# Rows of three feed-forward chunks and four attention pairs are moved as words into tiles of the rounded type before TensorE transposes them

## The reference, cut to what matters

```python
def swiglu(h, w1, w3, w2):                       # three times in all; hidden width 2816
    return (jax.nn.silu(h @ w1) * (h @ w3)) @ w2

def stick_breaking_attention(q, k, v):           # 16 heads of 64, blocks of 128 queries
    ...
        z = jnp.einsum('bthd,bshd->bhts', qb, k).astype(jnp.float32) * (HEAD_DIM ** -0.5)
        brk = jnp.where(strict, jax.nn.softplus(z), 0.0)
        ...
        log_a = jax.nn.log_sigmoid(z) - remain
        a = jnp.where(strict, jnp.exp(log_a), 0.0).astype(v.dtype)
        o = jnp.einsum('bhts,bshd->bthd', a, v)
```

## Time and profile before

| what | value |
|---|---|
| median of three runs | 950.38 us |
| profiled execution | 951.45 us |
| its span | 949.6 us |
| PE busy | 941.2 us, 99% of the span |
| DVE busy | 793.8 us, 84% |
| ACT busy | 578.3 us, 61% |
| granted TensorE clock | 1.00 |

### The profile page before, as it was taken

How to read it: one execution, slowest core, us unless ns; L and a number is a source line. 1 busy time by engine, 2 the same in 40 slices (tenths; PEclk the granted TensorE clock), 3 DMA queues, 4 the chain that set the end, 5 groups by cost and what they waited for, 6 DMA issues and landing times.

```text
span 949.6 us, 12028 instructions
## 1 busy us (share of the span) xinstructions
PE 941.2 (99%) x4705; PEld 785.0 (83%) x4705; DVE 793.8 (84%) x836; ACT 578.3 (61%) x609; POOL 86.9 (9%) x94
## 2 busy tenths in 40 slices
PE   7999999999999999999999999999999999999998
PEld 7877888888889888888888888888888888888887
DVE  4888999989856877999989888965885779999996
ACT  6666676665654655676666666565744456665672
POOL 3611101101010000101101023001010001101010
PEclk9999999999999999999999999999999999999999
DMA  8746888785457437879786367457255485987751
GB/s 297 269 134 202 253 295 236 190 298 134 145 125 249 153 114 220 244 249 259 202 278 164 114 155 251 171 181 218 94 199 196 165 273 141 318 236 208 255 133 44
DMA packets 125993, 191.32 MB, mean 201 GB/s; under 512 B 7353, under 2 KB 87617, under 8 KB 125937
## 3 DMA queue, kind: packets, MB, share of 16 engines
q1 hardware_dynamic: 110992, 172.59, 54.7%
q0 software_dynamic: 14640, 17.77, 10.6%
q10 hardware_dynamic: 304, 0.20, 0.1%
HBM read 189.49 MB, written 1.05 MB: 201 GB/s over the span
## 4 chain that ended last, share of the span: by engine, by line
PE 98%; ACT 1%; DMA 0%; DVE 0%; issue 0%; DVEq 0%
PE psum L2153 27%; PE psum L2154 26%; PE psum L2158 26%; PE psum L2297 4%; PE psum L2146 2%; PE psum L2148 2%; PE psum L2147 2%; PE psum L2671 1%; PE psum L2682 1%; PE psum L2672 1%; PE psum L2705 1%; PE psum L2731 1%; ACT arena L944 1%; PE psum L2334 0%; DMA cst<-consts 0%; PE psum L2314 0%
## 5 line engine op out<-in xcount | busy, mean ns | idle before, releaser
L1416 DVE TENSOR_TENSOR low<-raw,high 128x2048 fp32r<-128x2048 f32 (+1 forms) x109 | 245.4, 2253 | 60.2 <-ACT high L874 60.2
L874 ACT ACTIVATE high<-raw 128x2048 fp32r<-128x2048 f32 (+1 forms) x112 | 211.6, 1890 | 90.5 <-PE psum L2158 68.0
L2153 PE MATMUL psum<-high,xh 128*128 128x512 f32 x596 | 237.0, 398 | 0.0
L2154 PE MATMUL psum<-high,xl 128*128 128x512 f32 x596 | 232.6, 390 | 0.0
L879 ACT ACTIVATE high<-arena 128x2048 fp32r<-128x2048 f32 x88 | 168.7, 1917 | 75.9 <-PE psum L2158 72.2
L1422 DVE TENSOR_TENSOR low<-arena,high 128x2048 fp32r<-128x2048 f32 x88 | 200.7, 2286 | 11.1 <-ACT high L879 11.0
L2158 PE MATMUL psum<-low,xh 128*128 128x512 f32 x596 | 155.4, 390 | 0.0
L2153 PEld LDWEIGHTS psum<-high,xh 128*128 128x128 f32 x596 | 112.0, 188 | 23.3 <-issue 0.7
L2158 PEld LDWEIGHTS psum<-low,xh 128*128 128x128 f32 x596 | 111.6, 188 | 23.7 <-issue 0.3
L2154 PEld LDWEIGHTS psum<-high,xl 128*128 128x128 f32 x596 | 112.0, 188 | 22.1
L2153 PE MATMUL psum<-high,mh 128*128 128x512 f32 x256 | 102.1, 399 | 0.0
(11 more groups left out here) (241 smaller groups left out, 1185.6 us busy)
## 6 DMA issues: line engine op xcount, KB each, us to landing
raw<-in_ffn_w SPq DMA_DIRECT2D x68, 512.0 KB, 6.3
arena<-in_ffn_w SPq DMA_DIRECT2D x64, 512.0 KB, 7.0
raw<-in_w_in SPq DMA_DIRECT2D x50, 512.0 KB, 4.7
raw<-in_od_w_qkv SPq DMA_DIRECT2D x24, 512.0 KB, 5.0
raw<-in_w_ffn_down SPq DMA_DIRECT2D x22, 512.0 KB, 5.7
arena<-in_ffn_w POOLq DMA_DIRECT2D x16, 512.0 KB, 7.6
arena<-in_w_ffn_gate SPq DMA_DIRECT2D x16, 512.0 KB, 6.7
arena<-in_w_ffn_up SPq DMA_DIRECT2D x16, 512.0 KB, 8.2
```

The source lines that it names most:

```text
L874: nc.scalar.activation(high[:, n % RING, 0:cols], raw[:, r, 0:cols], ACT.Copy).then_inc(high_ready, 1)
L1416: nc.vector.tensor_tensor(low[:, n % RING, 0:cols], raw[:, RING_AT[n] % RING, 0:cols], high[:, n % RING, 0:cols].bitcast(F32), ALU.subtrac ...
L2153: nc.tensor.matmul(out, sh, wh, start=start, stop=False, skip_group_check=True)
L2154: nc.tensor.matmul(out, sl, wh, start=False, stop=False, skip_group_check=True)
```

## The change

Three feed-forward chunks (1, 6, 7, in each of the three feed-forwards) and four of the eight pairs of the stick-breaking attention (0, 1, 2, 6) are no longer transposed as fp32. SP copies their rows bit for bit into a tile of type fp32r (`words`, and `a_words`, which lies in the feed-forward's `gh`, idle at that time), and PE transposes that tile against `identr`, an fp32r copy of the identity that ACT makes once, ahead of the first feed-forward. The transposes themselves stay 128x128, four or six in a group.

Some of them stand elsewhere now. `hiddenT(1)` goes from in front of product 5 to behind product 2 of the first pair, `hiddenT(7)` from in front of product 5 to behind product 6 of the last, and `stick_aT` of pairs 0, 1, 2 and 6 goes from the start of unit 7+p to unit 8 (start), 8, 9 and 13 (in the middle, behind eight products of the unit). DVE's product of the next pair waits for the copy of this one instead of its transposes. Apart from that, the three semaphores of the constants become one, and so do those of the identity and the first gain.

```diff
+        MOVED_CHUNKS = (1, 6, 7)
...
-        A_T_BEFORE = {7 + p: p for p in range(8)}
+        A_T_BEFORE = {8: 0, 10: 3, 11: 4, 12: 5, 14: 7}
+        A_T_MID = {8: 1, 9: 2, 13: 6}
+        MOVED = (0, 1, 2, 6)
...
+            def move_a(p):
+
+                sp.wait_ge(a_ready, p + 1)
+                if p != MOVED[0]:
+                    sp.wait_ge(aT_ready, MOVED[MOVED.index(p) - 1] + 1)
+                sp.dma_start(a_words.bitcast(F32), o_a).then_inc(a_moved, 16)
...
+                def move_hidden(c):
+
+                    if c in PLAIN:
+                        sp.wait_ge(hidden_ready, 2 * plain_seq(f, c) + 2)
+                    else:
+                        sp.wait_ge(pair_hidden, 4 * pair_seq(f, c) + 4)
+                    before = MOVED_CHUNKS.index(c)
+                    if before:
+                        sp.wait_ge(hiddenT_ready, down_seq(f, MOVED_CHUNKS[before - 1]) + 1)
...
+                    for t in range(NT):
+                        sp.dma_start(words[:, t, :].bitcast(F32), hidden_of(c)[t]).then_inc(hidden_moved, 16)
...
                 load_down(f, 1)
+                move_hidden(1)
...
                 load_x21(7)
+                move_hidden(6)
...
                 load_down(f, 10)
+                move_hidden(7)
...
                 if n == U_Q:
-                    load_consts("bands", "bands", bands_in)
+                    load_consts("bands", "bands", masks_in)
                 if n == U_Q + 1:
-                    load_consts("rope", "rope", rope_in)
+                    load_consts("rope", "rope", masks_in)
...
+                if n - U_QKV[0] - 11 in (0, 1, 2):
+                    move_a(n - U_QKV[0] - 11)
...
+            nc.scalar.activation(identr[:], ident, ACT.Copy).then_inc(identr_ready, 1)
             ffn(0)
...
             dve.wait_ge(idx_w_copied, 2)
-            dve.wait_ge(masks_in, 16)
+            dve.wait_ge(masks_in, 16 * 3)
...
+                if p - 1 in MOVED:
+                    dve.wait_ge(a_moved, 16 * MOVED.index(p - 1) + 16)
+                elif p:
                     dve.wait_ge(aT_ready, p)
...
+                    if c in MOVED_CHUNKS:
+                        pe.wait_ge(hidden_moved, chunks_moved(f, c))
+                        pe.wait_ge(identr_ready, 1)
+                        for k in range(2):
+                            for t in range(NT):
+                                j = NT * k + t
+                                ins = nc.tensor.transpose(bank(6, j * P, (j + 1) * P).bitcast(F32R), words[:, t, k * P:(k + 1) * P], identr[:])
...
                 def products_6_2_3(p):
...
                     product(p, 6, bank(7), sum_tile(2), True, False)
+                    if p == LAST_PAIR:
+                        hiddenT(7)
                     pe.wait_ge(s1_ready, pairs_done(f, p))
                     product(p, 2, bank(0), x_tile(0, 1), False, True)
+                    if p == FIRST_PAIR:
+                        hiddenT(1)
...
-                pe.wait_ge(a_ready, p + 1)
+                if p in MOVED:
+                    pe.wait_ge(a_moved, 16 * MOVED.index(p) + 16)
+                    pe.wait_ge(identr_ready, 1)
+                else:
+                    pe.wait_ge(a_ready, p + 1)
```

More of the change, by code:

```diff
@@ L255, in program @@
         cst = sb("cst", [P, DECAY_AT])
+        identr = sb("identr", [P, P], F32R)
+        words = sb("words", [P, NT, FC], F32R)
         selbias = sb("selbias", [P, TRI])
@@ L359, in program @@
         o_a = take(2 * TRI).rearrange("p (e n) -> p e n", e=2)
+        a_words = gh.rearrange("p a b n -> p (a b n)")[:, 0:2 * TRI].rearrange("p (e n) -> p e n", e=2)
         A_RING = 4
@@ L386, in program @@
         r_o = xn
-        ident_in, masks_in, bands_in, rope_in = sem("ident_in"), sem("masks_in"), sem("bands_in"), sem("rope_in")
+        ident_in, masks_in = sem("ident_in"), sem("masks_in")
         decay_in = sem("decay_in")
         x_in = [[sem(f"x_in{t}_{q}") for q in range(2)] for t in range(NT)]
-        first_gain_in, gains_in = sem("first_gain_in"), sem("gains_in")
+        gains_in = sem("gains_in")
         first_gain_T, first_gain_ready = sem("first_gain_T"), sem("first_gain_ready")
@@ L448, in program @@
         stored, last_read = sem("stored"), sem("last_read")
+        identr_ready, a_moved, hidden_moved = sem("identr_ready"), sem("a_moved"), sem("hidden_moved")
         def bank(b, c0=0, c1=512):
@@ L572, in hidden_of, with chunks_moved @@
             return (f_half, f_C21[:, 0:FC]) if c in PAIRS else (f_C12[:, 0:FC], f_C22[:, 0:FC])
+        MOVED_CHUNKS = (1, 6, 7)
+        def chunks_moved(f, c):
+            return 32 * (len(MOVED_CHUNKS) * f + MOVED_CHUNKS.index(c) + 1)
         def landed_count(n):
@@ L666, in load_x21 @@
                     up_quarter(f, X21, p, 1, x21_in)
+                def move_hidden(c):
[6 more added lines that the diff above has]
+                        sp.wait_ge(hiddenT_ready, down_seq(f, MOVED_CHUNKS[before - 1]) + 1)
+                    elif f:
+                        sp.wait_ge(hiddenT_ready, down_seq(f - 1, MOVED_CHUNKS[-1]) + 1)
+                    for t in range(NT):
+                        sp.dma_start(words[:, t, :].bitcast(F32), hidden_of(c)[t]).then_inc(hidden_moved, 16)
                 load_up(f, 0, 0)
+                if f == 1:
+                    move_a(6)
                 load_up(f, 0, 1)
@@ L1143, in _ @@
             act.dma_start(ident, consts[:, 0:P]).then_inc(ident_in, 16)
[L1144 removed]
+            act.dma_start(gains[0:KD, 0:P], NORM_G[0].rearrange("(k p) -> k p", k=KD)).then_inc(ident_in, 16)
             def first_x_high(kk):
@@ L1277, in _ @@
                     stick_sigmoids(WEIGHTS_AT[u])
+                if u in A_T_MID:
+                    stick_aT(A_T_MID[u])
                 if u:
@@ L2047, in _ @@
                     s = chunk_set(unit)
-                    dve.wait_ge(rope_in, 16)
+                    dve.wait_ge(masks_in, 16 * 3)
                     for t in range(NT):
@@ L2350, in hiddenT @@
                         pe.wait_ge(gl_ready, down_seq(f, c))
+                    if c in MOVED_CHUNKS:
[5 more added lines that the diff above has]
+                                ins = nc.tensor.transpose(bank(6, j * P, (j + 1) * P).bitcast(F32R), words[:, t, k * P:(k + 1) * P], identr[:])
+                        ins.then_inc(hiddenT_ready, 1)
+                        return
                     rows = hidden_of(c)
@@ L2495, in first_x_T @@
                         ins.then_inc(first_xT, 1)
-            pe.wait_ge(ident_in, 16)
-            pe.wait_ge(first_gain_in, 16)
+            pe.wait_ge(ident_in, 16 * 2)
             nc.tensor.transpose(bank(FIRST_GAIN_BANK, 0, KD), gains[0:KD, 0:P], ident[0:KD, 0:KD]).then_inc(first_gain_T, 1)
@@ L2559, in pooling @@
                 pe.wait_ge(rel_ready, 1)
-                pe.wait_ge(bands_in, 16)
+                pe.wait_ge(masks_in, 16 * 3)
                 for g in range(4):
@@ L2730, in stick_aT @@
                     for j in range(3):
-                        ins = nc.tensor.transpose(bank(A_T_BANK + e, j * P, (j + 1) * P), o_a[:, e, j * P:(j + 1) * P], ident)
+                        dst = bank(A_T_BANK + e, j * P, (j + 1) * P)
+                        if p in MOVED:
+                            ins = nc.tensor.transpose(dst.bitcast(F32R), a_words[:, e, j * P:(j + 1) * P], identr[:])
+                        else:
+                            ins = nc.tensor.transpose(dst, o_a[:, e, j * P:(j + 1) * P], ident)
                 ins.then_inc(aT_ready, 1)
```

5 lines of the change are left out of this document (2 added, 3 removed).

## The result

The changed kernel takes 956.41 us (median of six runs, 954.79 to 957.42), the kernel before 950.37 us: a ratio of 1.0061, with an interval of 1.0050 to 1.0071. That is slower, and above the range that I gave (948.0 to 952.0). Its profiled execution took 955.59 us, with a span of 953.8 us, against 951.45 and 949.6.

A forecast was written before the change was run, and what follows sets the result against it. PE was taken as the bound, busy for 941.2 of 949.6 us. Transposes −1.97, masks +0.9 and attention pairs +0.15 give −0.92 us, so 949.5 us against the median, with a range of 948.0 to 952.0.

The forecast's parts named there:

- Chunk 7 is ready at 227.65, SP's queue is free from 224.89, ... 6.5 us, hidden too: Feed-forward: chunk 7's copies, taken as 2 to 4 us, land before PE wants them at 234.2; cost nothing.
- the sum: Whole kernel: −1.97 (transposes) + 0.9 (masks) + 0.15 (attention pairs) = −0.92 us; feed-forward copies priced at nothing.
- late rows: Rival, chance 0.06: copies inside the buffer take 8 us, pairs 1, 2 and chunk 7 come late; about +11 us, 961.
- Transposes: PE's 47 steps inside thirteen groups: 0.067 us each in the rounded type, 0.042 less than fp32; gain 1.97 us.
- I leave that step as it is: PE, from a group's last transpose to the first product behind it: taken as unchanged, no cost.
- load-bound: Rival, chance 0.15: the weight load sets the transposes' pace, steps of 0.109 to 0.120 us; 951.4 to 951.9 us.
- a floor for narrow products: Rival, chance 0.06: a narrow rounded product takes as long as 512 columns, 0.226 us; steps lose 5.5 us, 956.9.
- Masks: Start of top-k on DVE: the merged semaphore makes it wait for the rotation tables until 33.9; PE loses 0.9 us.
- Pairs of the stick-breaking attention: Stick-breaking attention: copies for pairs 1 and 2 may land late, 0 to 0.7 and 0 to 1.4 us; taken as 0.15.
- Chunks 1 and 6, the identity, the first gain: Feed-forward copies of chunks 1 and 6 hidden; merged identity and gain semaphore costs nothing, as PE waited for both already.
- no difference: Whole kernel: a time between 948.5 and 952.3 us, not told from no change; chance 0.70.

The follow-up runs named there:

- experiment 2: The changed kernel with SP issuing chunk 7's copy ahead of the four weight loads for chunks 9 and 10: 949.99 us, 0.9994 of the kernel before.
- experiment 4: The kernel before with one edit, masks, bands and rotation tables sharing one semaphore that top-k waits for: 951.75 us against 950.68, 1.0017.

## Why the prediction was wrong

The step that failed is "Chunk 7 is ready at 227.65, SP's queue is free from 224.89, ... 6.5 us, hidden too", and in it the bounds of 2 and 4 us for the copies. I asked whether SP could issue the copy, and it could. I did not ask what the DMA engines still had to move. The row for that stood in the trace of the kernel before, in the DMA issues from 222.0 to 225.2, and I had not read it:

```profile
q0 software_dynamic: 444, 0.45, 99.9%
...
raw<-in_ffn_w SPq DMA_DIRECT2D x4, 512.0 KB, 9.3
arena<-in_ffn_w POOLq DMA_DIRECT2D x1, 512.0 KB, 14.8
```

The first line says that POOL's packets took the engines in that stretch and none of SP's moved. SP's loads, issued at 222.3 to 224.9, took 9.3 us in the median, so they land at about 234, which is when PE comes; a copy issued behind them had little chance to be in time. It took 7.8 us where the sum had 2 to 4, so PE waited 2.66, 1.28 and 1.33 us where the sum had nothing. The prices that I took for the copy, from the end of the kernel and from an idle stretch, are prices without a backlog. The rival "late rows", at a chance of 0.06, had the right place and nearly the right price for chunk 7: 8 us for the copy, 1.5 us of wait three times. That was luck, since it took every copy as slow, by no cause that a row showed, and had pairs 1 and 2 as its main part; their copies land in 2.5 to 3.1 us.

The other steps, one by one:
- **Transposes**: forecast −1.97 us, measured −1.03. The steps inside a group were nearly right. By the starts of the single transposes in the trace of experiment 2 they are 0.069 to 0.070 us in groups of four and 0.075 to 0.078 in groups of six, against the forecast 0.067; in the kernel before, 0.108 and 0.109. With means of 0.069 and 0.076 they give 27 × 0.039 + 20 × 0.033 = 1.7 us. The term that was mis-sized is the step behind a group, of which the prediction says "I leave that step as it is". From the last transpose to a full product it was 0.03 us in fp32 and is 0.08 to 0.09 now; over the thirteen groups, that gives 0.7 us back. Why this step is longer no run shows. Both rivals on a slower step (load-bound, a floor for narrow products) are out.
- **Masks**: forecast +0.9 us, measured +1.07 alone. In the changed kernel's profile 0.4 of it shows. The landing of the tables and the two places where PE waits were right, but the size is partly luck. In experiment 4 DVE waited 2.5 us for the tables instead of 1.6, since the work ahead of top-k ran 0.9 us earlier in that execution. The three steps behind the first one of top-k gave 0.9 us back (1.13 us there, 2.04 before), which the sum did not have.
- **Pairs of the stick-breaking attention**: forecast +0.15, measured nothing. No PE wait names `gh`, and its copies land in 2.5 to 3.1 us.
- **Chunks 1 and 6, the identity, the first gain**: nothing, as forecast.

With the forecast's other terms as measured, −1.03 + 1.07 = 0.0 us: experiment 2 is that kernel, and measured 0.9994. So the forecast "no difference" was right for everything but chunk 7, though with half of the gain that it counted on. Chunk 7 added 5.3 us of waits, and half of the executions were some 2 us longer still at a lower clock.

## What to carry to other kernels

For a new transfer, two questions are needed: when its queue can issue it, and what has been issued shortly before by any queue and not yet landed. The time to landing of those neighbours, read in the trace of before, is nearer to the price of the new one (9.3 us there, 7.8 measured) than the price of such a transfer alone (2.1 us); a small copy that is needed soon belongs ahead of a large load that isn't. And where semaphores are merged, each waiter pays for the last of the landings.

## What the runs showed of the hardware that I had not expected

- A copy inside the chip's buffer was held up by transfers issued before it on other queues: it took 7.7 us on ACT's queue and 7.8 us on SP's own, with SP's same 2 MB and a load of POOL's ahead.
- A wait of 7.1 us of PE was followed by about 5 us at half the granted clock, about 1.8 us more; the two waits of 0.5 us in the even mixer's output projection leave the clock at 1.00, and so do the waits of 1.1 to 2.5 us in the changed kernel's profiled execution.
- Transposes of 128x128 in the rounded type run at 0.069 to 0.078 us from start to start, fp32 ones at 0.109 us. The Trainium skill, TensorE: Matmul & The Clock Gate, section "Back-to-back issue gap", gives about 81 ns for a stream of loads and 128-column products: the groups of six (0.075 to 0.078 us) come close to it. By the same page's section "LDWEIGHTS (loading the stationary operand)" a load of 128 columns would take 107 ns; the steps here are shorter, so that figure does not set their pace.
